# Opening and convolution of a two-layer diffusion backbone: new order of turns, two modulation chunks on VectorE, taps of two tiles in turn

## The chip, the cores and the metric

The kernel runs on one core of a Trainium2 chip. The metric is the device time of one execution in microseconds; three runs of the kernel before took 1659.43 to 1661.87 us, median 1660.55 us.

## What is computed

One sample with 512 latent tokens and 256 context tokens, D_MODEL = 1024, fp32, passes two layers. This case touches the start of layer 0: the modulation from the conditioning vector, the normalised and modulated input, the combined input projection and the depthwise convolution.

```python
silu_c = jax.nn.silu(c); silu_cc = jax.nn.silu(c_ctx)
mod = jnp.split((silu_c @ ada_w[l] + ada_b[l])[:, None, :], 6, axis=-1)      # 1024 x 6144 weights
mod_c = jnp.split(silu_cc @ ada_w[l] + ada_b[l], 6, axis=-1)
h = modulate(rms_norm(x, mix_pre_g[l]), mod[0], mod[1])                      # h * (1 + scale) + shift
hc = modulate(rms_norm(xc, mix_pre_g[l]), mod_c[0], mod_c[1])
p = h @ w_in; pc = hc @ w_in                                                 # conv | gates | q, k, v, o

def conv_module(glu_in, dw_w, ln_g, ln_b):
    a, b = jnp.split(glu_in, 2, axis=-1)
    u = a * jax.nn.sigmoid(b)
    u = dwconv(u, dw_w)                      # 31 taps, depthwise, over positions
    u = layer_norm(u, ln_g, ln_b)
    return jax.nn.silu(u)
```

The mLSTM group, the attention layer and two ConvFFNs follow; the change leaves their work as it is.

## The kernel before, in words

The program is raw: each engine (SP for the DMA queue, TensorE, ScalarE, VectorE, GpSimd) has its own list of instructions, written out by hand, and counting semaphores order them. An engine runs its list strictly in order, so an instruction that waits holds all that are behind it.

**High and low parts.** Products in fp32 are made of three matmuls: each operand is split into a high part (ScalarE, `take_high` for weights) and the rest (VectorE, `take_low`), and the matmuls are high x high, high x low, low x high. A weight granule is 128 x 4 x 256 values, 512 KB. It is loaded into one of two slots of `raw` (`load` waits until the granule two before has its low part), split into one of four slots of `w_hi` and `w_lo`, and used. `product` takes two granules (k = 0 to 3, then 4 to 7) and is one unit: two 128-column tiles over all 768 tokens. ScalarE splits granules n+4 and n+5 once the unit of granules n and n+1 is through. The semaphore `low` counts finished low parts, and `product` waits on it for each granule.

**The opening.** SP loads identity, c and c_ctx, six token tiles of x, and eight chunks `ada_0` of 1 MB each (1024 rows x 256 columns of the modulation weights) into a ring of six; ScalarE issues 19 small DMAs for vectors (`vrows`) before it does anything else. TensorE turns the vectors first (L816), then for each token tile j it turns the normalised tile (8 transposes, L816) and sums chunk j (`ada_0_sums`, L838, 16 matmuls with cond as weights), then chunks 6 and 7. Two chunks give a pair p of k-tiles with shift and scale; ScalarE copies their row (`ada_0_rows`, L1313), TensorE turns it into columns (`ada_0_cols`). ScalarE squares x and takes roots (L1178, L1181), VectorE normalises (`x_normed`, L1649, L1651) and copies the turned tokens out of PSUM (L1830). Then, pair by pair, VectorE makes the modulation vectors (L1595, L1858) and scales xT in place (L1864, four instructions a pair), ScalarE takes the high part (L1318), GpSimd the low part (L2282), and the first product waits for each k by `h0_ready`. VectorE's first `unit_low(0)` stands behind the third pair.

**The input projection.** The units are conv (4), gate (1, half width), qkov (7), two for turns, o (1). Beside the first four VectorE does `ada_sums` for two more chunks of the modulation (L1610, L1616). `gate_inputs` multiplies two tiles by the sigmoid. `conv_tile` is 31 instructions over 783 positions of one 128-channel tile (L1888, then L1890 30 times); each reads what the one before wrote and waits for it, and at given taps a `unit_low` for coming granules stands between. The rows of the mLSTM gates are scanned between tiles 1 and 2 (L1909 to L1931, ending in `rows_ready`, on which SP waits before it stores them and loads on).

## Time and profile before

| | |
|---|---|
| median of three runs | 1660.55 us |
| profiled execution | 1657.77 us, span 1656.1 us |
| TensorE matmul / weight load | 1606.8 us (97%) / 1345.1 us (81%) |
| VectorE | 1032.6 us (62%) |
| ScalarE | 552.9 us (33%) |
| GpSimd | 39.0 us (2%) |
| DMA | 169.43 MB, mean 102 GB/s |
| first matmul of the input projection | 59.44 us |

Times in the profile are microseconds from the span's start. PE is TensorE, PEld its weight load, DVE VectorE, ACT ScalarE, POOL GpSimd, SP the queue that issues DMAs. The profiled execution is one execution, 2.8 us under the median of the others; the span is the part of it that the trace covers.

### The profile page before, as it was taken

Reading aid. Unit: us, or ns where it says so; the run is one execution under the profiler, and the core shown is the slowest. Engines: PE = TensorE matmul, PEld = TensorE weight load, DVE = VectorE, ACT = ScalarE, POOL = GpSimd, SP = SyncE. Lnnn points to the kernel's source line nnn. Section 1 sums busy time; section 2 is a strip of 40 time slices with the busy share of each in tenths; the row PEclk is TensorE's granted clock in tenths of the full one; section 3 lists DMA queues with packets and bytes.
Section 4 is the critical chain, followed back from the end, with each engine's and each line's share of the span. In section 5 each row is a group of like instructions: output and inputs, shape, how many; then the busy total and the mean of one; then the engine's idle time right before and its main releaser. Section 6 shows DMA issues by size and latency. Waiting matters only on the chain.

```text
span 1656.1 us, 21947 instructions
## 1 busy us (share of the span) xinstructions
PE 1606.8 (97%) x8698; PEld 1345.1 (81%) x8698; DVE 1032.6 (62%) x1477; ACT 552.9 (33%) x883; POOL 39.0 (2%) x64
## 2 busy tenths in 40 slices
PE   5999999999999999999999999899999999999998
PEld 2688888777898887888888887788887988888886
DVE  2899996668747775566725446754885544454345
ACT  3313123665643221122311224622326432232133
POOL 0500000110000000000000000000000000000000
PEclk9999999999999999999999999999999999999999
DMA  9321212325116552456324222130002233223222
GB/s 311 129 76 53 78 51 70 115 96 127 39 51 209 179 185 87 140 166 203 117 86 140 77 77 77 55 127 26 1 11 80 89 102 115 79 88 114 88 92 85
DMA packets 134009, 169.43 MB, mean 102 GB/s; under 512 B 15970, under 2 KB 92450, under 8 KB 133930
## 3 DMA queue, kind: packets, MB, share of 16 engines
q1 hardware_dynamic: 133360, 168.11, 31.8%
q8 instruction: 55, 0.90, 0.2%
q10 hardware_dynamic: 570, 0.22, 0.1%
q14 instruction: 24, 0.20, 0.0%
HBM read 166.17 MB, written 2.15 MB: 102 GB/s over the span
## 4 chain that ended last, share of the span: by engine, by line
PE 88%; DVE 5%; ACT 3%; issue 1%; DVEq 0%; POOL 0%; ACTq 0%
PE acc L702 49%; PE acc L751 22%; PE acc L728 4%; PE acc L1135 2%; PE acc L915 2%; PE acc L1066 2%; PE acc L816 1%; PE acc L950 1%; PE acc L1081 1%; PE acc L670 1%; DVE w_lo L1595 1%; PE acc L894 1%; PE acc L742 0%; DVE h_lo L1595 0%; PE acc L1024 0%
## 5 line engine op out<-in xcount | busy, mean ns | idle before, releaser
L702 PE MATMUL acc<-h_hi,w_hi 128*128 128x512 f32 (+1 forms) x1424 | 417.3, 354 | 7.2 <-DVE w_lo L1595 4.2
L702 PE MATMUL acc<-h_lo,w_hi 128*128 128x512 f32 (+1 forms) x1424 | 413.0, 351 | 0.0
L702 PE MATMUL acc<-h_hi,w_lo 128*128 128x512 f32 (+1 forms) x1424 | 412.3, 351 | 0.0
L1595 DVE TENSOR_TENSOR w_lo<-raw,w_hi 128x1024 fp32r<-128x1024 f32 x183 | 219.7, 1230 | 147.0 <-ACT w_hi L1155 147.0
L702 PEld LDWEIGHTS acc<-h_hi,w_hi 128*128 128x128 f32 x1424 | 230.7, 189 | 45.0 <-issue 7.8
L702 PEld LDWEIGHTS acc<-h_lo,w_hi 128*128 128x128 f32 x1424 | 231.2, 189 | 38.6 <-issue 0.5
L702 PEld LDWEIGHTS acc<-h_hi,w_lo 128*128 128x128 f32 x1424 | 230.2, 189 | 38.1
L1155 ACT ACTIVATE w_hi<-raw 128x1024 fp32r<-128x1024 f32 x183 | 186.6, 1055 | 223.1 <-PE acc L751 173.9
L751 PE MATMUL acc<-w_hi,hid_hi 128*128 128x512 f32 x440 | 175.8, 400 | 0.0
L751 PE MATMUL acc<-w_lo,hid_hi 128*128 128x512 f32 x440 | 174.9, 397 | 0.0
L751 PE MATMUL acc<-w_hi,hid_lo 128*128 128x512 f32 x440 | 174.9, 397 | 0.0
L1890 DVE SCALAR_TENSOR_TENSOR conv_u<-conv_u,dw_w 128x783 f32<-128x783 f32 x120 | 124.2, 1035 | 4.0
L2118 DVE TENSOR_SCALAR hid<-gpad,ffn_cw 128x512 f32 (+1 forms) x66 | 25.2, 438 | 123.5 <-ACT gpad L1491 123.5
L751 PEld LDWEIGHTS acc<-w_hi,hid_lo 128*128 128x128 f32 x440 | 83.2, 189 | 20.4
L751 PEld LDWEIGHTS acc<-w_lo,hid_hi 128*128 128x128 f32 x440 | 83.3, 189 | 19.9
L751 PEld LDWEIGHTS acc<-w_hi,hid_hi 128*128 128x128 f32 x440 | 83.3, 189 | 19.9
L1595 DVE TENSOR_TENSOR hid<-hid,acc 128x1024 f32 (+3 forms) x22 | 32.7, 1488 | 107.1 <-ACT mods L1171 55.2
L2116 DVE SCALAR_TENSOR_TENSOR hid<-gpad,ffn_cw,hid 128x512 f32 (+3 forms) x132 | 77.6, 658 | 0.0
L1171 ACT ACTIVATE mods<-acc,vec 128x1 f32 (+2 forms) x72 | 14.4, 262 | 183.1 <-PE acc L670 183.1
L1491 ACT ACTIVATE gpad<-acc 128x1024 f32<-128x1024 f32 (+1 forms) x33 | 28.0, 887 | 118.0 <-PE acc L702 94.3
L751 PE MATMUL acc<-w_hi,h_hi 128*128 128x512 f32 x160 | 63.6, 397 | 1.0 <-DVE w_lo L1595 1.0
L751 PE MATMUL acc<-w_hi,h_lo 128*128 128x512 f32 x160 | 62.5, 390 | 0.0
(249 smaller groups left out, 2036.2 us busy)
## 6 DMA issues: line engine op xcount, KB each, us to landing
ada_w<-in_ada_w SPq DMA_DIRECT2D x88, 512.0 KB, 5.7
raw<-in_ffn_w_in SPq DMA_DIRECT2D x88, 512.0 KB, 3.7
raw<-in_ffn_w_out SPq DMA_DIRECT2D x44, 512.0 KB, 4.2
raw<-in_even_w_in SPq DMA_DIRECT2D x24, 512.0 KB, 4.5
ada<-in_ada_w SPq DMA_DIRECT2D x8, 1024.0 KB, 12.1
raw<-in_odd_w_in SPq DMA_DIRECT2D x12, 512.0 KB, 4.2
raw<-in_even_w_out SPq DMA_DIRECT2D x8, 512.0 KB, 4.7
ada_m<-in_ada_w SPq DMA_DIRECT2D x8, 512.0 KB, 4.3
```

Source lines behind the costliest of these rows:

```text
L702: last = nc.tensor.matmul(acc[:, s, m, t0:t1], w[:, slot, kk, c], x_[:, k, t0:t1], start=(k == 0 and q == 0), stop=(k == KD - 1 and q == 2))
L728: last = nc.tensor.matmul(acc[:, s, m, t0:t1], w_of(m_)[w][:, kk, c], x_[:, k, t0:t1], start=(k == 0 and q == 0), stop=(k == KD - 1 and q ...
L751: last = nc.tensor.matmul(tile_bank(name, a, j), x_[:, k, j * P:(j + 1) * P], w[:, m_ % 4, 2 * kk:2 * kk + 2, :].rearrange("p a c -> p (a ...
L915: last = nc.tensor.matmul(dst, probs[e % 4][:, t * P - t0:t * P - t0 + P], v_tok[:, ORDER[q], hd, :], start=(q, d, t) == FIRST_TOUCH[b], s ...
L1066: last = nc.tensor.matmul(acc[:, 0, n % 2, t0:t1], inb[:, 2 + hd, i * P:(i + 1) * P], kT[:, hd // 3, t0:t1], start=True, stop=True)
L1135: last = nc.tensor.matmul(acc[:, 1, 1, c:c + P], v1[:, j, (hd // 3) * HD:(hd // 3 + 1) * HD], pT[:, n % 2, j * P:(j + 1) * P], start=(j == ...
L1155: nc.scalar.activation(dst, raw[:, n % 2], ACT.Copy).then_inc(high, 1)
L1491: last = nc.scalar.activation(gpad[:, :, c:c + t1 - t0], acc[:, u % 2, :, t0:t1], ACT.Copy)
L1595: return nc.vector.tensor_tensor(out_, in0, in1, op)
L1890: ins = nc.vector.scalar_tensor_tensor(dst, src, tap, dst, ALU.mult, ALU.add)
L2116: ins = nc.vector.scalar_tensor_tensor(dst, src, c, dst, ALU.mult, ALU.add)
L2118: ins = nc.vector.tensor_scalar(dst, src, c, None, ALU.mult)
```

## The change

In the opening:
- ScalarE issues the first ten vector DMAs, SP the other nine, behind x. TensorE turns the vectors after the fourth token, into columns of the ada bank; ScalarE takes them out later (`take_vectors`).
- TensorE turns tokens 0 and 1, sums chunk 0, turns 2 and 3, sums chunk 1, turns the vectors and tokens 4 and 5, and then does chunks 4, 5, 6, 7. Chunks 2 and 3 (pair 1) are summed over k by VectorE (`ada_1_sums`, 32 instructions of 128x256 in two alternating chains) and reduced over partitions by eight one-column matmuls (`ada_1_cols`). The load order is 0, 1, 2, 4, 3, 5, 6, 7; the last comes behind the first granule of w_even. Pair 3's columns are turned inside the first product, ahead of k = 1.
- ScalarE in place of VectorE copies the turned tokens out of PSUM, one instruction a token.
- VectorE scales xT into tiles of its own (`h_32`), and ScalarE makes the high part from the unscaled xT, with shift and scale in the same instruction, two a k. VectorE in place of GpSimd makes the low part (`first_low`). `take_high` and `take_low` of the first two granules stand one by one between them.
- GpSimd clears only the pads of conv_u.

In the convolution `conv_pair` takes the taps of two tiles in turn; each instruction waits for the one before the last. The positions of the `unit_low` calls follow, with 16 now behind the row scans. One tile's result goes to a tile of its own (`conv_e`), and h_tok and sq_junk move to other addresses.

The diff, cut to its core (the helpers `take_vectors` and `turn_token` hold the moved copies and transposes; in the rest of the diff `conv_t[t]` replaces `conv_u[:, t]`):

```diff
+OPENING = (0, 1, 2, 4, 3, 5, 6, 7)
...
+        conv_e = place("conv_e", [P, U_LEN], offset=W_EDGE + 1024)
+        conv_t = [conv_u[:, 0, :], conv_e[:, :], conv_u[:, 1, :], conv_u[:, 2, :]]
+        h_tok = place("h_tok", [P, NT, P], offset=(U0 + 3 * U_LEN * 4 + 31) // 32 * 32)
...
+        def load_vectors(eng, first, end):
+            for q in range(first, end):
+                block_, src = vectors[q]
+                r = sum(v.shape[0] for b, v in vectors[:q] if b == block_)
+                eng.dma_start(vrows[r:r + src.shape[0], block_, :], src).then_inc(sem("vec_in"), 16)
...
+            load_vectors(sp, 10, N_VECTORS)
             def load_ada_0(first, end):
-                for o in range(first, end):
+                for pos in range(first, end):
+                    o = OPENING[pos]
                     c = o // 2 + 4 * (o % 2)
-                    if o >= 6:
-                        sp.wait_ge(ada0_sums, o - 5)
-                    sp.dma_start(ada_0[:, o % 6], w_ada[0][:, :, c * 256:(c + 1) * 256]).then_inc(ada0_in[o], 16)
-            load_ada_0(0, 6)
+                    if pos >= 6:
+                        sp.wait_ge(ada0_sums, pos - 5)
+                    sp.dma_start(ada_0[:, pos % 6], w_ada[0][:, :, c * 256:(c + 1) * 256]).then_inc(ada0_in[o], 16)
+            load_ada_0(0, 7)
             n = G["conv"]
...
             load(sp, n, w_even[:, 0:4, 512:768])
-            load_ada_0(6, 7)
+            load_ada_0(7, 8)
             load(sp, n + 1, w_even[:, 4:8, 512:768])
-            load_ada_0(7, 8)
...
+            def turn_vectors():
+                pe.wait_ge(sem("vec_in"), 16 * N_VECTORS)
+                for b, (n, col) in enumerate(((92, 0), (84, 92), (66, 176), (66, 242), (124, 308))):
+                    last = transpose(acc[:, v % 2, 0, 512 + col:512 + col + n], vrows[0:n, b, :], n)
+                last.then_inc(unit_done, 1)
...
+            def ada_1_cols():
+                pe.wait_ge(ada1_sums, 1)
+                psum_free(pe, v)
+                for c in range(2):
+                    for q in range(2):
+                        for x_ in range(2):
+                            at_ = 512 + 4 * c + 2 * q + x_
+                            last = nc.tensor.matmul(acc[:, v % 2, 0, at_:at_ + 1], ada_p1[:, x_, c, q * P:(q + 1) * P],
+                                                    ones[:, 0:1], start=True, stop=True)
+                last.then_inc(ada1_cols, 1)
...
+            turn_token(0)
+            turn_token(1)
+            ada_0_sums(0)
+            turn_token(2)
+            turn_token(3)
+            ada_0_sums(1)
+            turn_vectors()
+            turn_token(4)
+            turn_token(5)
+            ada_0_cols(0)
+            ada_0_sums(4)
+            ada_0_sums(5)
             ada_0_sums(6)
             ada_0_cols(2)
             ada_0_sums(7)
-            ada_0_cols(3)
+            ada_1_cols()
             h = (h_hi, h_lo)
+            def first_ready(k):
+                if k == 1:
+                    ada_0_cols(3)
+                pe.wait_ge(h0_ready, k + 1)
             for j in range(4):
-                product(pe, U["conv"] + j, G["conv"] + 2 * j, h, always if j else lambda k: pe.wait_ge(h0_ready, k + 1),
+                product(pe, U["conv"] + j, G["conv"] + 2 * j, h, always if j else first_ready,
...
+            def turned_token(j):
+                u = U["xt"]
+                if j < NT - 1:
+                    act.wait_ge(xt_full, j + 1)
+                else:
+                    psum_full(act, u)
+                nc.scalar.activation(xT[:, :, j * P:(j + 1) * P], acc[:, u % 2, j % 2, :].rearrange("p (k t) -> p k t", k=KD),
+                                     ACT.Copy).then_inc(xt_taken if j < NT - 1 else set_free[u % 2], 1)
...
+            def ada_0_rows(p):
+                act.wait_ge(ada0_sums, (2, 0, 4, 6)[p])
+                if p:
+                    act.wait_ge(ada0_cols, p - 1)
+                c = 512 * (p % 2)
+                nc.scalar.activation(ada_r[0:2, :], acc[0:2, U["ada"] % 2, p // 2, c:c + 512], ACT.Copy).then_inc(ada0_rows, 1)
+            def first_high(p):
+                act.wait_ge(mods0, p + 1)
+                for k in (2 * p, 2 * p + 1):
+                    for s_, (t0, t1) in enumerate(SEGS[T]):
+                        last = nc.scalar.activation(h_hi[:, k, t0:t1], xT[:, k, t0:t1], ACT.Identity,
+                                                    bias=mods[:, 0, 0, k, s_:s_ + 1], scale=mods[:, 0, 1, k, s_:s_ + 1])
+                    last.then_inc(t_high, 1)
...
+                if j >= 2:
+                    turned_token(j - 2)
             ada_0_rows(0)
-            ada_0_rows(1)
+            take_vectors()
+            turned_token(NT - 2)
+            turned_token(NT - 1)
+            psum_read(act, U["xt"])
             first_high(0)
             ada_0_rows(2)
+            take_high(0)
+            ada_0_rows(3)
+            take_high(1)
             first_high(1)
-            unit_high(0)
-            ada_0_rows(3)
             first_high(2)
             first_high(3)
             unit_high(2)
...
+            def ada_1_sums(e):
+                o = 2 + e
+                dve.wait_ge(ada0_in[o], 16)
+                for k in range(KD):
+                    for x_ in range(2):
+                        w, scale, of = ada_0[:, OPENING.index(o) % 6, k, :], cond[:, k, x_:x_ + 1], ada_p1[:, x_, e, :]
+                        if not k:
+                            ins = nc.vector.tensor_scalar(of, w, scale, None, ALU.mult)
+                        else:
+                            sd.wait(sd.value() - 1)
+                            ins = nc.vector.scalar_tensor_tensor(of, w, scale, of, ALU.mult, ALU.add)
+                        if e and k == KD - 1 and x_:
+                            ins.then_inc(ada1_sums, 1)
+                        else:
+                            sd.done(ins)
...
+            def first_mods(p):
+                u = U["ada"]
+                k = slice(2 * p, 2 * p + 2)
+                if p == 3:
+                    psum_full(dve, u)
+                elif p == 1:
+                    dve.wait_ge(ada1_cols, 1)
...
-                        last = nc.vector.tensor_scalar(xT[:, kk, t0:t1], xT[:, kk, t0:t1], mods[:, 0, 1, kk, s:s + 1],
+                        last = nc.vector.tensor_scalar(h_32[kk][:, t0:t1], xT[:, kk, t0:t1], mods[:, 0, 1, kk, s:s + 1],
                                                        mods[:, 0, 0, kk, s:s + 1], ALU.mult, ALU.add)
                     last.then_inc(t_ready, 1)
-                if p == 2:
-                    unit_low(0)
+            def first_low(p):
+                for k in (2 * p, 2 * p + 1):
+                    dve.wait_ge(t_ready, k + 1)
+                    dve.wait_ge(t_high, k + 1)
+                    vt(h_lo[:, k, :], h_32[k][:, :], h_hi[:, k, :].bitcast(F32), ALU.subtract).then_inc(h0_ready, 1)
+            for j in range(NT):
+                if j >= 2:
+                    dve.wait_ge(xt_full, j - 1)
+                x_normed(j, j)
+            psum_read(dve, U["cond"])
+            ada_1_sums(0)
+            psum_read(dve, U["vec"])
+            psum_read(dve, U["xt"])
+            first_mods(0)
+            ada_1_sums(1)
+            first_low(0)
+            take_low(0)
+            first_mods(1)
+            first_low(1)
+            first_mods(2)
+            first_low(2)
+            take_low(1)
+            first_mods(3)
+            first_low(3)
             unit_low(2)
...
-            def conv_tile(t, lows):
+            def conv_pair(t, lows):
                 dve.wait_ge(sem("sig_used"), t // 2 + 1)
-                dst = conv_u[:, t, HALF:HALF + taps_len]
+                sd.wait()
                 for w in range(TAPS):
-                    src = conv_u[:, t + 1, w:w + taps_len]
-                    sd.wait()
-                    tap = dw_w[:, w, t:t + 1]
-                    if w == 0:
-                        ins = nc.vector.tensor_scalar(dst, src, tap, None, ALU.mult)
-                    else:
-                        ins = nc.vector.scalar_tensor_tensor(dst, src, tap, dst, ALU.mult, ALU.add)
-                    sd.done(ins)
                     if w in lows:
                         unit_low(lows[w])
+                    for t_ in (t, t + 1):
+                        src, dst = conv_u[:, t_ + 1, w:w + taps_len], conv_t[t_][:, HALF:HALF + taps_len]
+                        tap = dw_w[:, w, t_:t_ + 1]
+                        if w == 0:
+                            sd.done(nc.vector.tensor_scalar(dst, src, tap, None, ALU.mult))
+                        else:
+                            sd.wait(sd.value() - 1)
+                            sd.done(nc.vector.scalar_tensor_tensor(dst, src, tap, dst, ALU.mult, ALU.add))
                 sd.wait()
             ada_sums(EVEN[0], sums_even[0])
             ada_sums(EVEN[1], sums_even[1])
             psum_read(dve, U["conv"] + 1)
             gate_inputs(0)
-            conv_tile(0, {2: 6, 13: 8, 30: 10})
+            conv_pair(0, {0: 6, 9: 8, 15: 10, 21: 12, 28: 14})
             psum_read(dve, U["conv"] + 3)
             gate_inputs(2)
-            conv_tile(1, {8: 12, 20: 14, 30: 16})
...
-            unit_low(18)
-            conv_tile(2, {13: 20, 29: 22})
-            conv_tile(3, {13: 24, 29: 26})
+            unit_low(16)
+            conv_pair(2, {4: 18, 13: 20, 21: 22, 29: 24})
             nc.vector.tensor_copy(mark[:, 2:3], ident[:, 0:1]).then_inc(sem("conv_done"), 1)
+            unit_low(26)
...
-                pool.wait_ge(t_high, k + 1)
-                nc.gpsimd.tensor_tensor(h_lo[:, k, :], xT[:, k, :], h_hi[:, k, :].bitcast(F32), ALU.subtract).then_inc(h0_ready, 1)
             pool.wait_ge(h0_ready, KD)
-            nc.gpsimd.memset(conv_u[:, :, :], 0.0).then_inc(sem("conv_zero"), 1)
+            for first, end in ((0, U_LAT), (U_LAT + LAT, U_CTX), (U_CTX + CTX, U_LEN)):
+                ins = nc.gpsimd.memset(conv_u[:, :, first:end], 0.0)
+            ins.then_inc(sem("conv_zero"), 1)
```

## Rows read from the trace of the kernel before

**Rows 1.** The page, totals and the chain that ended last.
```profile
PE 1606.8 (97%) x8698; PEld 1345.1 (81%) x8698; DVE 1032.6 (62%) x1477; ACT 552.9 (33%) x883; POOL 39.0 (2%) x64
...
PE 88%; DVE 5%; ACT 3%; issue 1%; DVEq 0%; POOL 0%; ACTq 0%
```

**Rows 2.** Table by stage: each engine's busy time, granted clock, DMA.
```profile
core 0: us, PE busy (x) PEld busy (x) DVE busy (x) ACT busy (x) POOL busy (x), PEclk, DMA share, GB/s
17.89:59.44 41.55, 38.37 (x193) 17.75 (x193) 24.65 (x42) 15.47 (x27) 8.57 (x5) 1.00 0.57 183
59.44:78.20 18.76, 18.76 (x97) 16.21 (x98) 16.73 (x17) 3.52 (x4) 12.65 (x5) 0.91 0.75 242
78.20:259.50 181.30, 181.30 (x1041) 157.56 (x1040) 174.20 (x183) 46.22 (x51) 0.00 (x0) 1.00 0.23 69
62.00:63.00 1.00, 1.00 (x4) 0.81 (x4) 0.96 (x2) 0.00 (x0) 1.00 (x2) 0.50 1.00 338
```

**Rows 3.** Timeline of TensorE: start, length, instruction, count, idle before and releaser.
```profile
16.02 0.98 PE L816 MATMUL acc<-ident,vrows 92*128 92x92 f32 x5 [12.26 <-DMA vrows<-in_conv_dw_w]
...
19.79 5.24 PE L838 MATMUL acc<-ada,cond 128*2 128x256 f32 x16
24.96 1.09 PE L816 MATMUL acc<-ident,xn 128*128 128x128 f32 x8
25.99 3.61 PE L838 MATMUL acc<-ada,cond 128*2 128x256 f32 x16
...
44.93 7.07 PE L838 MATMUL acc<-ada,cond 128*2 128x256 f32 x32
```

**Rows 4.** The chain in order of time: start, length, engine and line.
```profile
57.04 2.40 issue
59.44 35.69 PE acc L702 x192
95.12 1.68 PE acc L670 x16
```

**Rows 5.** Timeline of VectorE, 46 to 60 us.
```profile
46.83 1.65 DVE L1864 TENSOR_SCALAR xT<-xT,mods 128x512 f32<-128x512 f32 x4
...
48.78 4.55 DVE L1864 TENSOR_SCALAR xT<-xT,mods 128x512 f32<-128x512 f32 x4
...
58.12 2.35 DVE L1595 TENSOR_TENSOR w_lo<-raw,w_hi 128x1024 fp32r<-128x1024 f32 x2
```

**Rows 6.** DMA from 0 to 75 us in 40 slices, and x's loads.
```profile
GB/s 2 109 349 363 407 409 345 325 333 348 348 347 348 349 348 348 348 348 348 351 321 81 0 0 0 0 4 0 0 4 0 0 175 347 357 399 366 227 145 225
...
L480 SPq DMA_DIRECT2D x<-in_ctx x2: 504/514/524, 3.8 to 4.4; - x2
...
DMA to landing us min/median/max: 4.3/6.7/9.2
```

**Rows 7.** ScalarE: a copy out of PSUM, grouped, and squares from the timeline.
```profile
L1345 ACT ACTIVATE conv_u<-acc 128x1024 f32<-128x1024 f32 x2 | 2.1, 1038 | 13.1 <-PE acc L702 13.1
...
19.08 1.04 ACT L1178 ACTIVATE junk<-x 128x1024 f32<-128x1024 f32 x1
...
20.45 1.04 ACT L1178 ACTIVATE junk<-x 128x1024 f32<-128x1024 f32 x1
```

**Rows 8.** VectorE: groups (count, busy us, mean ns) and timeline of ada chains and taps.
```profile
L1890 DVE SCALAR_TENSOR_TENSOR conv_u<-conv_u,dw_w 128x783 f32<-128x783 f32 x120 | 124.2, 1035 | 4.0
...
L1616 DVE SCALAR_TENSOR_TENSOR ada_c<-ada_w,cond,ada_c 128x512 f32<-128x512 f32 x28 | 19.3, 747 | 0.6
...
87.23 9.94 DVE L1616 SCALAR_TENSOR_TENSOR ada_c<-ada_w,cond,ada_c 128x512 f32<-128x512 f32 x14
...
105.95 11.75 DVE L1890 SCALAR_TENSOR_TENSOR conv_u<-conv_u,dw_w 128x783 f32<-128x783 f32 x11
```

**Rows 9.** Timelines of VectorE and ScalarE around the convolution.
```profile
99.00 1.97 DVE L1595 TENSOR_TENSOR conv_u<-conv_u,sig_b 128x512 f32<-128x512 f32 x4 [1.83 <-ACT conv_u L1345]
...
182.04 0.94 DVE L1909 SCALAR_TENSOR_TENSOR rows<-rows 8x768 f32<-8x768 f32 x1
...
195.12 2.34 DVE L1595 TENSOR_TENSOR w_lo<-raw,w_hi 128x1024 fp32r<-128x1024 f32 x2
...
191.69 1.46 ACT L1369 ACTIVATE qkov<-acc 128x1536 f32<-128x1536 f32 x1 [13.61 <-PE acc L702]
```

137 lines of the change are left out of this document (41 added, 96 removed).

## Prediction

> **What bounds the kernel now.** The page's totals come first [rows 1]: the reader is to see TensorE busy for 97% of the span and the chain that ended last lying on it for 88%. Work taken from another engine counts only where TensorE stands and waits for it. The table by stage says where that is [rows 2]: from 17.89 to 59.44 us TensorE is nearly full (38.37 of 41.55), but with preparation; from 59.44 us on, in the first input product, and from 78.20 to 259.50 us it has no idle time at all. So what happens before the first product moves the end one for one, unless later work comes too late for TensorE.
>
> The timeline of TensorE [rows 3] shows the preparation: vector turns at 16.02 us after 12.26 us of waiting for the last vector's DMA, token turns of 1.03 us (24.96 to 25.99), and eight modulation chunks of 3.54 us each (two in 7.07). The chain [rows 4] has 2.40 us put down to issue just ahead of the first product. VectorE's first w_lo ends them (58.12 [rows 5] plus one of two at 1.18 us gives 59.3), so the last step is not TensorE's. VectorE's own rows [rows 5] say why it is late: four scalings take 1.65 us at 46.83 and 4.55 us at 48.78, when GpSimd works on h_lo.
>
> **The opening, step by step, in the order of the new program.**
> ScalarE issues 10 vector DMAs in place of 19, so it starts some 3 us earlier; SP issues the other nine behind x, while x is still arriving. Tokens 0 and 1 are turned at about 10 to 14 us. Then TensorE waits for the first ada chunk. The DMA rate is flat at 348 GB/s [rows 6]; x, identity and vectors are 3.44 MB, so the first chunk's bytes are through at 15.5 us, and x itself landed some 1.4 us behind its bytes (the last at most 9.2 us after an issue at 4.4): I take 17.
>
> From there TensorE's list, with the prices of rows 3: first chunk 5.2 (as slow as now), two turns 2.1, second chunk 3.55, vectors 1.0, two turns 2.1, four row transposes 0.35, chunks o = 4, 5, 6 10.65, transposes 0.35, chunk 7 3.55, and eight column matmuls for the pair computed on VectorE, 0.85 (16 take 1.68 [rows 4]). Sum 29.7, hence 46.7 us. Two chunks (7.1 us) are gone, the waits at both ends besides. The last chunk's bytes are through at 38.2 us by the same rate, with w's first granule in front: not limiting by 4 us or more, and the two ring waits on SP are met at 22 and 28 us while DMA still has over 3 us queued.
>
> Do the others keep up? ScalarE now copies the turned tokens: 128x1024 out of PSUM is 1.04 us, squares with root 1.37 us per token (19.08 to 20.45) [rows 7]. Its copy of token 2 ends at 24.5, squares of token 5 at 26, token 5's xn at 27.1, before TensorE wants it at 30. VectorE loses its copies out of PSUM and gets 32 partial-sum steps on 128x256. No row has this shape. The same operation on 128x512 in two alternating chains takes 0.71 us start to start (14 in 9.94) [rows 8]; 271 more elements cost 0.288 us (1035 against 747 ns), so 256 fewer make 0.44; the first step of each chain is a tensor_scalar, 0.31 as an estimate under the 0.41 that one of 384 columns takes on average at 46.83 [rows 5]. A chunk is 14 x 0.44 + 2 x 0.31 = 6.8 us; the bounds are 5 us (at 0.3 a step) and 11.4 us (at the 512 price). VectorE: first chunk 27.2 to 34.0, modulation and four scalings to 36.0 (1.65 us, since GpSimd now has no h_lo), second chunk to 42.8, first_low(0) two at 0.9 to 44.7, first take_low to 45.9. That is 0.8 us before TensorE's 46.7, the tightest meeting of the opening. ScalarE's take_high(0) follows the rows at 38.4 and ends at 40.
>
> Then products: k = 0 to 48.8, the last row transposes (0.35), k = 1 to 51.3. Meanwhile VectorE gets the pair's columns at 46.7 and has k = 2's low part at 49.7, 3's at 50.6, 4's at 53.4, 5's at 54.4, and take_low(1) at 55.6, which the second half of the product wants at 55.5: 0.1 us. Parts 6 and 7 come at 58.5 and 59.4, wanted at 59.8 and later. ScalarE's affine high parts run beside VectorE's scalings instead of behind them; 512 and 256 columns at some 0.95 us a k (three quarters of the 1.04, and a second start) stay ahead of first_low. Without a stall this product takes 17.0 us plus 0.4; now it takes 18.76, of which the surplus is a stretch at the lower clock: the granted clock was 0.50 (1.2 GHz) at 62 us [rows 2], behind 2.40 us in which TensorE stood. The new order leaves no such stand. So product 0 ends at 64.1 instead of 78.20: **14.1 us gained**. GpSimd's memset of the pads alone, after 59.4, is hidden: ScalarE asks for it at 64.
>
> **The convolution.** It is all on VectorE, off the path; what counts is when each w_lo between the taps is ready. Per tap now: 11 in 11.75, 1.068 us start to start, with each waiting for the one before. The alternating ada chains start 0.037 us ahead of the previous duration's end (0.71 against 747 ns) where the serial taps start 0.033 behind (1.068 against 1035 ns) [rows 8]. I take 1.00 for a tap in turn; bounds 0.95 and 1.07. 124 taps give back 8 us of VectorE, which buys nothing by itself.
>
> The Trainium skill ("VectorE: DVE Perf Modes", section "The DRAIN you can't avoid") says the flush behind each operation can't be skipped by dropping semaphores, which would make a tap in turn cost what a serial one does. Rows 8 already show two prices for the two ways of waiting, and the sum goes by them. By the page the conv term would be that of the first rival below.
>
> Now count from the end of the second product (now 96.8, then 82.7). VectorE leaves the opening at 62.3 (w_hi 3 waits for its load), does two ada_sums at 10.8 and a pair of w_lo at 2.35, and begins gate_inputs at +3.5, where it now begins at +2.2 (99.00) [rows 9]. Then gate_inputs 1.97, w_lo 6 and 7 2.35, 18 steps, w_lo 8, 12 steps, w_lo 10, 12 steps, w_lo 12, 14 steps, w_lo 14, 6 steps: +78.4. Each of these comes 1 us or more ahead of its product. Then gate_inputs 1.97 and the row scans 13.1 (182.04 to 195.12) [rows 9], and only now unit_low(16), which stood ahead of the scans until now: granule 16 is ready at +94.6, and its product starts at +94.9 (191.69 less 96.8). Margin 0.3 us, with the sum above uncertain by two; I count 0.3 us of stall. Later ones (18 at +102, 20 at +123, 22 at +142) meet 111.9, 128.9 and 145.8; the last, 26, waits for ScalarE as it does now. The loads behind them follow each w_lo by less than 9.2 us, the slowest landing of the 512 KB transfers in rows 6, and rows_ready, on which SP stands, comes 5 us earlier against the products (+93 for +98). From 260 us on nothing changes but places of tiles.
>
> **Sum.** 14.1 - 0.3 = 13.8 us. The profiled execution took 1657.77 us with a span of 1656.1; it becomes 1644.0. It lies 2.8 us below the median of the runs, so for the median: 1660.55 - 13.8 = **1646.8 us**.
>
> **Rivals.**
> *Taps gain nothing* (13%). Then granule 16 is late by 60 x 0.07 - 0.3 = 3.9 us, once, before the fourth qkov product; 14.1 - 3.9 = 10.2, hence 1650.4. For it: no row has taps in turn with these tiles. Against: rows 8.
> *VectorE bounds the opening* (9%). If a 128x256 step costs what a 128x512 one does, both chunks take 22.8 for 13.6 us, the first w_lo comes at 55.1, and 8.4 us of the gain are gone: 5.4 left, 1655.2. For it: no row has the shape. Against: 271 elements more cost 288 ns [rows 8].
> *TensorE stays at its lower clock* (6%), the case that ends slower. The first chunk takes 5.24 us where later ones take 3.61 [rows 3]; and in product 0 the granted clock fell to 0.50 behind a stand [rows 2]. The new order interrupts TensorE before the first chunk and puts short transposes between. A chunk at half the clock costs 3.5 us more; four of them use up the 14 us, and from there the kernel is slower: five chunks make 17.5, and with a third of product 0 (17 us more if all of it is at half the clock) 23, hence some 1670; 1665 in the middle of the case. Against: from 24.4 on there is no gap longer than those of now, where chunks took 3.54.
> *The gain is given back at a later wait* (3%), no change: nothing between 78 and 260 us shows a wait that doesn't move along.
>
> **How the numbers follow.** The forecast has 69%, with 1644 to 1649 as its own range: 1.6 us for the first chunk all at the slow pace, 2 for take_low's meetings and arrival of ada, 1.4 for the taps' margin, 1 for the median. The range goes to 1642.5 below (no stall, 1 us from earlier ada, scatter of runs of 1.2) and to 1653.5 above, which takes in the taps' case and part of the second. A measurement of this kernel can tell 0.2%, 3.3 us, from no change. Faster by more: forecast, taps, and nearly all of the second rival, 0.90; the same 0.04; slower 0.06.
>
> **What would show it.** In the new profile: the first L702 matmul at 46 to 48 us; six chunks with 3.5 us each behind the first; a granted clock of 1.00 through the first product, which lasts 17.4 us; 32 steps on VectorE at 0.44; taps at 1.00 start to start; a TensorE wait for w_lo of 0 to 1 us before the fourth qkov product; all that follows as long as before. I am wrong if that wait is 4 us, if the first product stands at k = 2 or 4, or starts after 50 us.

## The result, and the profile after

Kernels run together on one chip gave 1648.64 us (median of four runs, 1647.59 to 1650.08) for the changed kernel and 1660.41 us (1659.43 to 1661.87) for the one before: a ratio of 0.9935, 95% interval 0.9922 to 0.9948, or 11.8 us less. The forecast was 13.8 us less.

The page of the changed kernel, totals and the chain that ended last:
```profile
PE 1605.0 (97%) x8678; PEld 1349.0 (82%) x8678; DVE 1022.0 (62%) x1505; ACT 561.6 (34%) x896; POOL 18.0 (1%) x58
...
PE 91%; DVE 5%; ACT 2%; issue 1%; DMA 1%; SPq 0%; DVEq 0%; POOL 0%; ACTq 0%
```
Against [rows 1] TensorE's busy time is nearly the same; its share of the chain rose from 88 to 91%. VectorE is 10.6 us less busy and GpSimd 21 us less, and neither number says anything of the gain.

The table by stage, with the borders moved to where the same work stands now:
```profile
core 0: us, PE busy (x) PEld busy (x) DVE busy (x) ACT busy (x) POOL busy (x), PEclk, DMA share, GB/s
17.22:46.66 29.44, 29.44 (x158) 14.48 (x158) 18.73 (x45) 12.09 (x21) 0.00 (x0) 0.94 0.88 279
46.66:64.69 18.03, 18.03 (x104) 15.27 (x104) 17.26 (x32) 9.54 (x14) 0.36 (x3) 1.00 0.46 162
64.69:245.98 181.29, 181.29 (x1042) 157.66 (x1040) 175.65 (x196) 46.02 (x51) 0.00 (x0) 1.00 0.26 76
```
The third row is the comparison to begin with: 181.29 us here, 181.30 us for the same stretch in [rows 2], at 1.00. From the first product's end to the last qkov copy nothing was gained or lost. The gain lies ahead of it: the preparation takes 29.44 us and starts at 17.22, and TensorE has no idle time in it; the first product takes 18.03 where it took 18.76, at a granted clock of 1.00 for 0.91.

TensorE's timeline from the first token turns to the first product:
```profile
10.48 3.65 PE L843 MATMUL acc<-ident,xn 128*128 128x128 f32 x16 [6.65 <-DVE xn L1704]
17.22 5.30 PE L874 MATMUL acc<-ada,cond 128*2 128x256 f32 x16 [3.09 <-DMA ada<-in_ada_w]
22.45 1.97 PE L843 MATMUL acc<-ident,xn 128*128 128x128 f32 x16
24.35 3.61 PE L874 MATMUL acc<-ada,cond 128*2 128x256 f32 x16
27.90 0.60 PE L843 MATMUL acc<-ident,vrows 92*128 92x92 f32 x5
28.34 1.91 PE L843 MATMUL acc<-ident,xn 128*128 128x128 f32 x16
...
30.52 10.52 PE L874 MATMUL acc<-ada,cond 128*2 128x256 f32 x48
...
41.30 3.62 PE L874 MATMUL acc<-ada,cond 128*2 128x256 f32 x16
44.85 1.95 PE L894 MATMUL acc<-ones,ada_p 128*128 128x1 f32 x16
46.66 0.59 PE L729 MATMUL acc<-h_hi,w_hi 128*128 128x512 f32 x2
```
Read it by the starts; lengths overlap a little. There are six chunks of the modulation (16 + 16 + 48 + 16 matmuls) where [rows 3] had eight, and the only two waits stand ahead of 17.22. The first product, which stood at 59.44 [rows 4], starts at 46.66.

VectorE in the same time, with its two chunks:
```profile
26.94 0.61 DVE L1882 TENSOR_SCALAR ada_p<-ada,cond 128x256 f32<-128x256 f32 x2
27.46 5.63 DVE L1885 SCALAR_TENSOR_TENSOR ada_p<-ada,cond,ada_p 128x256 f32<-128x256 f32 x14
...
35.49 5.62 DVE L1885 SCALAR_TENSOR_TENSOR ada_p<-ada,cond,ada_p 128x256 f32<-128x256 f32 x14
...
42.77 1.22 DVE L1648 TENSOR_TENSOR w_lo<-raw,w_hi 128x1024 fp32r<-128x1024 f32 x1
46.83 0.17 DVE L1648 TENSOR_TENSOR mods<-acc,vec 128x8 f32<-128x8 f32 x1 [2.85 <-PE acc L894]
```
A step costs 0.40 us (5.63 / 14), and the first w_lo ends at 44.0, 2.7 us before TensorE asks. The [2.85 <-PE] in the last row says who leads: VectorE waits for TensorE's columns, not the other way.

The convolution's taps, and the pair of w_lo behind the row scans:
```profile
90.80 1.03 DVE L1969 SCALAR_TENSOR_TENSOR conv_u<-conv_u,dw_w 128x783 f32<-128x783 f32 x1
91.74 1.03 DVE L1969 SCALAR_TENSOR_TENSOR conv_e<-conv_u,dw_w,conv_e 128x783 f32<-128x783 f32 x1
92.69 1.03 DVE L1969 SCALAR_TENSOR_TENSOR conv_u<-conv_u,dw_w 128x783 f32<-128x783 f32 x1
...
173.44 2.34 DVE L1648 TENSOR_TENSOR w_lo<-raw,w_hi 128x1024 fp32r<-128x1024 f32 x2
```
A tap starts every 0.946 us (90.80 to 92.69 is two), against 1.068 in [rows 8], though one instruction is still recorded as 1.03 us. Granule 16 is ready at 174.65, one of the two in the last row.

ScalarE's copies of the qkov products show TensorE's pace, and when that granule is wanted:
```profile
178.14 1.46 ACT L1422 ACTIVATE qkov<-acc 128x1536 f32<-128x1536 f32 x1 [13.62 <-PE acc L729]
195.10 1.46 ACT L1422 ACTIVATE qkov<-acc 128x1536 f32<-128x1536 f32 x1 [13.54 <-PE acc L729]
```
The product with granule 16 begins where a copy begins, at 178.1: a margin of 3.5 us, and no wait for w_lo.

**Where the difference sits.** The same instruction on both traces, changed less before: first product's start -12.8 us, its end -13.5, every qkov copy from 144 to 246 us -13.6, the last copy of the stage (o, at 273.19) -13.7, then -12.0 at the first FFN's entry, -8.9 in layer 1 and to the end (the span -8.6). (The mark called o is ScalarE's copy of the last product of the stage.) The opening's gain reached 273 us whole, and 5 us of it seemed to be lost in two stages in which the change moves only the places of some tiles. That needed the first two runs.

### The profile page after: what moved, and what is told of

Same layout as the page of the kernel before. It is cut to its first block, busy times and chain, and to the rows that moved or that the text cites. A ratio compares the mean times of both kernels' runs of the same rounds, so it can differ in the third digit from the quotient of the medians.

```text
span 1647.5 us, 21953 instructions
## 1 busy us (share of the span) xinstructions
PE 1605.0 (97%) x8678; PEld 1349.0 (82%) x8678; DVE 1022.0 (62%) x1505; ACT 561.6 (34%) x896; POOL 18.0 (1%) x58
## 4 chain that ended last, share of the span: by engine, by line
PE 91%; DVE 5%; ACT 2%; issue 1%; DMA 1%; SPq 0%; DVEq 0%; POOL 0%; ACTq 0%
PE acc L729 49%; PE acc L778 22%; PE acc L755 4%; PE acc L970 2%; PE acc L1190 2%; PE acc L1121 2%; PE acc L843 2%; PE acc L874 1%; PE acc L1136 1%; PE acc L1005 1%; PE acc L697 1%; PE acc L983 1%; DVE w_lo L1648 1%; PE acc L949 1%; DMA ada<-in_ada_w 1%
## 5 line engine op out<-in xcount | busy, mean ns | idle before, releaser
L1969 DVE SCALAR_TENSOR_TENSOR conv_u<-conv_u,dw_w 128x783 f32<-128x783 f32 x90 | 87.8, 1020 | 0.0
## 6 DMA issues: line engine op xcount, KB each, us to landing
ada<-in_ada_w SPq DMA_DIRECT2D x8, 1024.0 KB, 11.8
```

Source lines behind the costliest of these rows:

```text
L1969: sd.done(nc.vector.scalar_tensor_tensor(dst, src, tap, dst, ALU.mult, ALU.add))
```

## The experiments

Twelve runs. `before_again` and `after_again` are the two kernels unchanged; the others are the changed kernel with the edit shown.

**1. Are the two late stages a loss?** (`before_again`)

> The kernel before, unchanged, profiled a second time. Theory 1 (the stretches at the lower TensorE clock fall and last differently in each execution): ratio 1.000 within 0.1%; the trace shows the same instructions at the same distances, but the summed time at a granted clock of 0.5, 28.6 us in the first trace, differs by 5 us or more, and the span follows it by half. Theory 2 (each kernel has its own stretches): the same stretches at the same places to 1 us, 28.6 us in sum.

Measured: 1660.76 us (ten runs), ratio 0.9998 [0.9988, 1.0007] to its own comparison runs; this trace has a span of 1660.6 us. The attention stage of layer 1 in three traces, the first kernel twice and then the changed one:
```profile
1071.50:1302.47 230.97, 222.97 (x1338) 186.55 (x1337) 153.01 (x247) 88.48 (x156) 0.00 (x0) 0.99 0.17 53
```
```profile
1072.55:1306.99 234.44, 226.45 (x1338) 189.30 (x1337) 153.03 (x247) 88.42 (x155) 0.00 (x0) 0.97 0.17 52
```
```profile
1059.54:1293.56 234.02, 226.02 (x1338) 189.23 (x1337) 153.08 (x247) 88.44 (x155) 0.00 (x0) 0.97 0.17 52
```
The counts are the same and the busy times of VectorE and ScalarE too; TensorE is 3.5 us longer busy in the second trace of the *unchanged* kernel, at 0.97 for 0.99. So the 3.0 us that the change seemed to cost there belong to the first trace of before, which was 2.6 us under the median of its runs. The time at the lower level of the clock (granted 0.50, 1.2 GHz) can be added up from the granted clock of windows of 2 us over the whole span: 28.7 us in that trace, 47.7 in this one, 45.8 in the changed kernel's (the next expectation has 47.9 for it). So the sum differed by 19 us between two executions of one kernel, well over the least 5 that was expected, but the span grew by 4.5 us, a quarter of that and not half.

**2. The changed kernel once more** (`after_again`)

> The changed kernel, unchanged, profiled a second time and timed in five rounds. Theory 1: ratio 0.9925 to 0.9935 (11 to 12.5 us), the sum at the lower clock, 47.9 us in the first trace, comes out nearer 35, and the span falls by half the difference; the first 277 us gain 13.6 as in the first trace. Theory 2 (the new kernel has more stretches of its own and gives 2 to 5 us back by them): 47.9 us again, at the same places.

Measured: 1649.62 us, 0.9934 [0.9921, 0.9948]; first product at 46.63, its end at 64.67, o at 273.33: the opening repeats within 0.2 us. The time at the lower clock, added up in the same way, was 48.1 us, not the smaller sum expected: that part missed.

**3. The opening alone** (`opening_only`): the taps one tile at a time, as before.
```diff
-            def conv_pair(t, lows):
+            def conv_tile(t, lows):
...
-            conv_pair(0, {0: 6, 9: 8, 15: 10, 21: 12, 28: 14})
+            conv_tile(0, {2: 6, 13: 8, 30: 10})
```

> The new opening with the old convolution: one tile after the other, each tap waiting for the last, the low parts at their old places. My theory: the opening carries the whole gain, the first product starts at 46.6 us, the end of the third qkov product is 13.6 us earlier than before; ratio within 0.05% of the changed kernel's. Granules 16 and 17 are then split ahead of the row scans: no wait of TensorE. Rival (the faster taps carry part, since VectorE comes later to the convolution): a wait of TensorE for w_lo of 1 to 4 us between 120 and 250 us, ratio 0.1 to 0.25% above the changed kernel's.

Measured: 1649.65 us, 0.9934 [0.9921, 0.9948], the whole change's ratio to the last digit. TensorE meets the end of the convolution late, though:
```profile
259.47 1.53 PE L949 MATMUL acc<-conv_u,ones 128*128 128x512 f32 x4 [1.40 <-DVE small L2011]
```
No wait was expected here, so that part missed, and it is tempting to call these 1.4 us what the faster taps buy. But this trace had TensorE at a faster pace (see the last section): its last qkov copy stands at 244.38 us, against 245.98 in the changed kernel, where the same matmul starts at 259.35 without a wait. VectorE let it go here at 259.47. At the changed kernel's pace some 0.1 us of the wait would be left, so that the taps buy next to nothing there, and o stands at 273.24 and 273.19 in the two traces.

**4. The convolution alone** (`conv_only`): the opening as before.
```diff
-            load_vectors(sp, 10, N_VECTORS)
...
-                for pos in range(first, end):
-                    o = OPENING[pos]
+                for o in range(first, end):
```

> The old opening with the new convolution: taps of two tiles in turn. My theory: taps start every 0.946 us instead of 1.068, VectorE has 15 us more, and the time stays as before: ratio 1.000 within 0.1%, since no low part was waited for before. Rival (VectorE's freed time or the moved low parts reach the path): a ratio below 0.999, or above 1.001 if granule 16, now behind the row scans, comes late for its product at 191.7 us.

Measured: 1661.31 us (eleven runs), 1.0002 [0.9993, 1.0011], and no TensorE wait at all from 60 to 259 us. A tap starts every 0.946 us here too, so 120 of them take some 15 us less of VectorE's time than at 1.068, in a stretch where TensorE never waited for it: nothing. Runs 3 and 4 together put the whole gain in the opening.

**5. All eight chunks on TensorE** (`chunks_on_pe`): the pair computed on VectorE goes back.
```diff
-OPENING = (0, 1, 2, 4, 3, 5, 6, 7)
+OPENING = (0, 1, 2, 3, 4, 5, 6, 7)
...
+            ada_0_sums(2)
+            ada_0_sums(3)
...
-                ada_1_cols()
```

> The changed kernel with all eight modulation chunks summed by TensorE, as before: chunks 2 and 3 and their columns stand behind the vector turns, the load order is 0 to 7. My theory (the opening is TensorE's list, and the pair on VectorE takes 7.1 us of it and gives 1.95 back by its columns): the first product starts 5.0 to 5.8 us later, at 51.7 to 52.5 us, and all later marks with it. Rival (VectorE's and ScalarE's chain sets the start, so that the pair on VectorE bought nothing): start at 46 to 48 us.

Measured: 1652.85 us (ten runs), 0.9955 [0.9942, 0.9969].
```profile
17.53 6.24 PE L874 MATMUL acc<-ada,cond 128*2 128x256 f32 x16 [3.32 <-DMA ada<-in_ada_w]
...
25.60 3.62 PE L874 MATMUL acc<-ada,cond 128*2 128x256 f32 x16
...
53.43 0.62 PE L729 MATMUL acc<-h_hi,w_hi 128*128 128x512 f32 x2
```
From the second chunk's start to the first product it is 27.83 us here and 22.31 (24.35 to 46.66) in the changed kernel: 5.52 us. That is two chunks at 3.55 and a set of row transposes at 0.33, less 1.81 for the eight column matmuls: 5.6. The rest of the later start, 1.25 us, is the first chunk, which came 0.3 us later and ran 0.9 us longer. In all the product starts 6.8 us later, where 5.0 to 5.8 were expected. Of the 12.8 us by which the first product starts earlier, 5.5 are the pair's; the other 7.3 belong to the rest of the new opening: no 12-us wait with a late preparation behind it, and no 2.40 us ahead of the product. No run takes those edits apart. In the medians the pair is worth 3.2 us (1652.85 and 1649.62), and at o 3.7: this trace ran its later products at 16.64 us each and not 16.96, which gave part of the late start back.

**6. Each tap waits for the last one again** (`pair_waits_last`), in the new order and with the new places.
```diff
-                            sd.wait(sd.value() - 1)
+                            sd.wait()
```

> The changed kernel; each tap of a pair waits for the instruction just before it instead of the one before the last. My theory (what a tap in turn saves is the wait for its forerunner's end): taps start every 1.068 us again instead of 0.946; the low part of granule 16 then comes 5.7 us later (7.3 less the 1.65 us that VectorE now waits for w_hi at 119.6) and TensorE waits some 2.3 us for it before the fourth qkov product at 178.1 us. Rival (the flush behind each VectorE instruction is paid either way, and the gain per tap came from the other tile's addresses): taps stay at 0.946 and no wait appears.

Measured: 1652.31 us in one run. VectorE, then TensorE at granule 16:
```profile
91.31 1.04 DVE L1969 SCALAR_TENSOR_TENSOR conv_u<-conv_u,dw_w 128x783 f32<-128x783 f32 x1
92.38 1.03 DVE L1969 SCALAR_TENSOR_TENSOR conv_e<-conv_u,dw_w,conv_e 128x783 f32<-128x783 f32 x1
```
```profile
180.46 0.60 PE L729 MATMUL acc<-h_hi,w_hi 128*128 128x512 f32 x2 [3.69 <-DVE w_lo L1648]
...
182.46 0.84 PE L729 MATMUL acc<-h_lo,w_hi 128*128 128x512 f32 x2
183.10 0.84 PE L729 MATMUL acc<-h_hi,w_lo 128*128 128x512 f32 x2
```
The step went from 0.946 to 1.070 us with nothing changed but which predecessor is waited for: 0.124 us a tap. And the first rival's mechanism exists: granule 16 is 3.69 us late, and behind the wait pairs of matmuls start 0.64 us apart for some 3 us, where they start 0.35 apart otherwise. The wait was expected shorter (2.3): TensorE came 1.3 us earlier, since it ran at the faster pace up to there (the copy before stands at 176.81, not 178.14); at the changed kernel's pace the wait would be some 2.4. The time of the one run can't show a loss of this size.

**7. GpSimd takes the opening's low parts again** (`low_on_gpsimd`).
```diff
-            first_low(0)
...
+            for k in range(KD):
+                pool.wait_ge(t_ready, k + 1)
+                pool.wait_ge(t_high, k + 1)
+                nc.gpsimd.tensor_tensor(h_lo[:, k, :], h_32[k][:, :], h_hi[:, k, :].bitcast(F32), ALU.subtract).then_inc(h0_ready, 1)
```

> The changed kernel with the first low parts on GpSimd, from the same scaled tiles. My theory (GpSimd beside VectorE slows both): VectorE's partial sums of the second chunk, 0.40 us a step, go to 0.6 or more while GpSimd works, and GpSimd's 1.9 us a k becomes 2.3 to 2.8 beside VectorE; the first product starts 0 to 2 us later and ends 1 to 4 us later. Rival (the move to VectorE bought nothing): both marks within 0.3 us of the changed kernel's 46.65 and 64.2 us.

Measured: 1649.4 us in one run; first product at 46.94, and it takes 19.44 us (18.03 in the changed kernel), with two waits in it, 0.7 for w_lo and 0.6 for h_lo. VectorE, then GpSimd:
```profile
35.25 3.73 DVE L1882 TENSOR_SCALAR ada_p<-ada,cond 128x256 f32<-128x256 f32 x2
38.90 5.62 DVE L1885 SCALAR_TENSOR_TENSOR ada_p<-ada,cond,ada_p 128x256 f32<-128x256 f32 x14
...
50.92 4.67 DVE L1916 TENSOR_SCALAR h<-xT,mods 128x512 f32<-128x512 f32 x4
```
```profile
35.20 3.63 POOL L2348 TENSOR_TENSOR h_lo<-h,h_hi 128x768 fp32r<-128x768 f32 x2 [34.26 <-ACT h_hi L1360]
```
Two tensor_scalars that take 0.61 us alone take 3.73 beside GpSimd's pair, which runs from 35.20 to 38.83: they end as it ends. The four scalings go from 1.65 to 4.67, as in [rows 5]. The long chain behind them keeps its 0.40 a step, so the slower steps that were expected there missed. Taking GpSimd out of the opening is worth 1.4 us in the first product by this trace; in the time of one run it doesn't show.

**8. The high parts from the scaled tiles** (`high_from_scaled`): ScalarE copies h_32 when VectorE has scaled it.
```diff
-                    for s_, (t0, t1) in enumerate(SEGS[T]):
-                        last = nc.scalar.activation(h_hi[:, k, t0:t1], xT[:, k, t0:t1], ACT.Identity,
...
+                    act.wait_ge(t_ready, k + 1)
+                    nc.scalar.activation(h_hi[:, k, :], h_32[k][:, :], ACT.Copy).then_inc(t_high, 1)
```

> The changed kernel; ScalarE takes the high part as a copy of the scaled tile, one instruction a k behind VectorE's scaling, instead of two with shift and scale from the unscaled tile. My theory (0.81 us a copy keeps pace with 0.82 us of scaling a k; the low part comes when it did): start and end of the first product within 0.3 us of the changed kernel's. Rival (the edit shortens the chain to h_lo by a scaling): the first product waits at k = 2 for 0.5 to 1 us and ends as much later.

Measured: 1652.38 us in one run. The first product takes 18.25 us, 0.2 more, with the same 0.3 us of wait for w_lo; it starts 0.6 us later, for a first chunk that took 6.14 us. The edit is worth between 0 and 0.2 us.

**9. Spare work ahead of the first chunk** (`warm`): 30 and 28 transposes of the identity into a bank nobody reads, ahead of token 0's turns and behind token 1's.
```diff
+            def warm(n):
+
+                for q in range(n):
+                    transpose(acc[:, v % 2, 1, 512:640], ident[:, :])
+
+            warm(30)
...
+            warm(28)
```

> The changed kernel with 30 spare 128x128 transposes of the identity on TensorE ahead of token 0 and 28 between token 1 and the first chunk, where it stands idle for 6.6 and 3.1 us. My theory (the first chunk takes 5.3 us in place of 3.6 because TensorE comes to it at its lower clock): turns of 1.03 us and a first chunk of 3.6 us, and the first product starts 1.4 to 1.7 us earlier than at 46.65. Rival (the first chunk is slow for its data still arriving, or TensorE's start is bounded elsewhere): 5.3 us again, or a start within 0.3 us.

Measured: 1645.96 us in one run; the first and the last chunk, and the product:
```profile
17.38 3.62 PE L874 MATMUL acc<-ada,cond 128*2 128x256 f32 x16 [0.51 <-DMA ada<-in_ada_w]
...
40.58 3.61 PE L874 MATMUL acc<-ada,cond 128*2 128x256 f32 x16 [0.73 <-DMA ada<-in_ada_w]
...
45.93 0.59 PE L729 MATMUL acc<-h_hi,w_hi 128*128 128x512 f32 x2
```
A TensorE that turned spare tiles up to 0.51 us before the first chunk, instead of standing for 3.09, runs it in 3.62 us instead of 5.30: what TensorE did before sets the price. In the changed kernel the granted clock agrees, 0.67 over the chunk (here 1.00), but not in every trace. The first chunk in the changed kernel and in `opening_only`:
```profile
17.22:22.45 5.23, 5.23 (x16) 1.63 (x16) 0.00 (x0) 0.00 (x0) 0.00 (x0) 0.67 1.09 348
```
```profile
17.59:23.70 6.11, 6.11 (x16) 1.79 (x16) 0.00 (x0) 0.00 (x0) 0.00 (x0) 1.00 1.09 348
```
The second is slower still, at a recorded 1.00, as are `chunks_on_pe` (6.17) and `high_from_scaled` (6.07), and the kernel before took 5.17 us at 1.00. So the run shows that the slow chunk comes from the stand; that the lower clock is all of it is not shown. Less came through (0.7 us): the last chunk's load, ordered behind w's first granule and a ring wait, is now what TensorE waits for.

**10. The first chunk ahead of x's last tokens** (`ada_early`).
```diff
+                if j == 2:
+                    load_ada_0(0, 1)
```

> The changed kernel with the first ada chunk loaded ahead of x's third tile instead of behind all of x and the vectors. My theory (the opening is TensorE's list from the first chunk's landing on): the first chunk starts at 14 us in place of 17.2, and what follows moves up by 3 us until the last chunk's landing (39.6 us) stops it: its sum starts at about 39.7 in place of 41.3, the first product at 45.1, 1.5 us earlier. Rival (another chain bounds the start): within 0.3 us of 46.65.

Measured: 1647.73 us in one run.
```profile
13.42 3.62 PE L874 MATMUL acc<-ada,cond 128*2 128x256 f32 x16
...
20.53 3.61 PE L874 MATMUL acc<-ada,cond 128*2 128x256 f32 x16 [1.60 <-DMA ada<-in_ada_w]
...
32.53 8.76 PE L874 MATMUL acc<-ada,cond 128*2 128x256 f32 x32 [2.22 <-DMA ada<-in_ada_w]
```
Starting 3.8 us earlier gained nothing: TensorE outruns the loads, waits 1.60 and 2.22 us, and behind the second the clock falls again (0.80 over the two chunks, which take 8.76 us for 7.07). The product starts at 46.91: the expected 45.1 was missed by 1.8.

**11 and 12. Both, and spare work with the last chunk's load first.** `early_order_warm` joins 9 and 10 and takes VectorE's chunk 3 after 5; `warm_last_first` is run 9 with
```diff
-            load_ada_0(0, 7)
+            load_ada_0(0, 8)
...
-            load_ada_0(7, 8)
```

> The changed kernel with three edits: the first ada chunk ahead of x's third tile, load order 0, 1, 2, 4, 5, 3, 6, 7 with both granules of w behind the last chunk, and 30 spare transposes ahead of token 0. My theory (landing times and TensorE's list share the bound): chunk 6 is summed from 35 us, chunk 7 to 42.3, the first product starts at 44.1 us, 2.5 us earlier than in the changed kernel, ratio 0.991 to 0.993. Rival (short waits for chunks 1 and 5 bring the lower clock back): chunks of 5 us or more behind these waits and a start after 46 us.

> The changed kernel with the 58 spare transposes of the previous run and with the last ada chunk loaded ahead of both granules of w instead of between them. My theory (the 0.73 us for which TensorE waited for the last chunk at 39.8 us goes, nothing else is late): chunk 7 starts behind its forerunners without a wait, the first product at 45.2 us, 1.4 us earlier than in the changed kernel; in time that is too little to show beside executions that differ by 2 us either way: ratio 0.991 to 0.994. Rival (the first granule of w, now later, holds the first product): a wait for w_lo and a start at 46 us or later.

Measured: `early_order_warm` 1650.01 us (six runs, 1646.94 to 1654.42), 0.9933 [0.992, 0.9947], first product at 45.34 (44.1 expected) with waits of 1.44 and 2.29 us for DMA on the way. The rival, chunks of 5 us behind these waits, didn't come:
```profile
36.11 3.62 PE L873 MATMUL acc<-ada,cond 128*2 128x256 f32 x16 [2.29 <-DMA ada<-in_ada_w]
```
So a stand of 2.29 us cost nothing here, where 2.22 us in `ada_early` cost 1.7; what makes the difference isn't shown. `warm_last_first` gave 1649.32 (1646.77 to 1650.83), 0.9926 [0.9913, 0.994]:
```profile
39.85 3.62 PE L873 MATMUL acc<-ada,cond 128*2 128x256 f32 x16
...
45.20 0.59 PE L728 MATMUL acc<-h_hi,w_hi 128*128 128x512 f32 x2
```
The last chunk doesn't wait, and the product starts at 45.20, as the sum had it: 1.4 us earlier than in the changed kernel, the earliest of all. In the time it can't be told from it (0.9926 and 0.9934, intervals overlapping). Its own trace shows a reason, behind o, at a load that the changed kernel's TensorE meets without waiting:
```profile
292.93 1.35 PE L989 MATMUL acc<-cond,ada_m 128*128 128x2 f32 x8 [1.31 <-DMA ada_m<-in_ada_w]
```
It came to o 1.29 us ahead of the changed kernel (271.90 and 273.19) and waits 1.31 us here; at the first FFN's entry nothing is left (487.18 and 487.13). In `early_order_warm` this wait is 0.28 us. That trace, the slowest of its six executions, has something larger in the same stage:
```profile
292.00:304.00 12.00, 11.98 (x50) 10.29 (x51) 3.82 (x6) 1.23 (x2) 0.37 (x2) 0.58 0.39 124
```
TensorE full for 12 us, with 50 matmuls at a granted clock of 0.58. The stage took 218.22 us in place of 213.94: such a stretch costs more than the opening had left to give.

Marks of the traces, in us (pace: from one qkov copy to the next; the last three are lengths from o on: to the first FFN, the two FFN stages with what is between, the attention stage):
```
kernel             product 0 starts  ends    pace    o        lengths
before                  59.44        78.24   16.96   286.90   212.20 572.40 230.97
before_again            58.97        77.50   16.96   285.69   212.92 573.94 234.44
conv_only               58.20        76.73   16.64   282.68   211.78 574.00 233.85
chunks_on_pe            53.43        70.99   16.64   276.93   212.04 573.97 234.45
opening_only            47.91        65.80   16.64   273.24   212.01 572.39 233.99
after                   46.66        64.69   16.96   273.19   213.94 572.41 234.02
after_again             46.63        64.67   16.96   273.33   213.73 574.75 234.00
warm                    45.93        63.97   16.96   272.62   214.30 572.40 230.93
early_order_warm        45.34        63.37   16.96   272.02   218.22 573.96 234.51
warm_last_first         45.20        63.24   16.96   271.90   215.28 573.99 233.95
```

## Why the prediction was right, step by step

**What bounds.** Right. What ended before the first product moved everything behind it up to o; the 181.29 us after it stayed to the hundredth. Runs 3 and 4 show the same from outside: opening alone 0.9934, convolution alone 1.0002.

**The first product's start: 46.7 expected, 46.66 measured.** The terms didn't all hold; their errors cancel, so that the match to 0.04 us is luck. From start to start: wait for the first chunk to 17.22 (17); first chunk 5.23 (5.2); two turns 1.90 (2.1); second chunk 3.55 (3.55); vectors 0.44 (1.0); two turns 1.84 (2.1); row transposes 0.34 and 0.33 (0.35); three chunks 10.45 (10.65); the last 3.55 (3.55); columns 1.81 (0.85). The mis-sized term is the last. Eight fp32 matmuls against a column of ones are 16 instructions in the trace, and they take 1.81 us, near the 1.68 that [rows 4] gave for 16: the row was there, but the count was taken from the source. The vectors' 1.0 came from a record's length (0.98), when what counts is the distance to the next start.

**VectorE: step 0.40, not 0.44**; a chunk 6.1 us, not 6.8; first take_low at 44.0, not 45.9. The second rival (9%), that VectorE bounds the opening, is out: it waits 2.85 us for TensorE. The loads were no limit in the change itself, but closer to one than counted: in run 9 the last chunk's data let TensorE go at 40.58, 0.7 us ahead of that chunk's start in the changed kernel (41.30), where the forecast had over 4 us (38.2 by bytes).

**Product 0: 17.4 expected, 18.03 measured.** 16.96 is the product, 0.33 the row transposes, 0.30 a wait for take_low(1) at 55.87 (0.1 was expected at 55.5), and 0.44 remains: some 0.3 for three restarts (after the columns, the row transposes and the wait), whose first pair of matmuls takes about 0.1 longer each (0.59 to 0.62, not 0.51), and 0.15 that no row explains. The granted clock was 1.00 as forecast: without the 2.40-us stand, no fall at 62 us. The third rival (6%) didn't come: chunks behind the first took 3.5. Its mechanism is real nevertheless: runs 6, 9 and 10 show 1.5 to 1.7 us behind a stand of 2 to 4 us. It isn't a fixed price, since in `early_order_warm` a stand of 2.29 us cost nothing.

So the term was 14.1 and came out at 13.5: the product's extra 0.6.

**The convolution: 0.3 us of stall expected, none measured.** The tap was taken at 1.00, between 0.95 and 1.07, and is 0.946. Sixty steps by 0.054 make the 3.2 us by which granule 16 beat the forecast (ready 91.4 us behind the second product's end, not 94.6). Whoever adds up the 62 steps of the forecast at 1.00 gets 79.2 and not its 78.4; it comes out with the two first steps, tensor_scalars, at some 0.6, which the forecast doesn't say. The first rival (13%) is settled by run 6, which is that rival built: a tap of 1.070 and a late granule, 3.69 us against the 3.9 in its sum. That the two are so near is luck again, since the pace of that trace made the wait 1.3 us longer. The rule of the Trainium skill that was weighed there ("VectorE: DVE Perf Modes", section "The DRAIN you can't avoid") would have priced both ways of waiting alike; here 0.946 and 1.070 us stand for the same 128x783 operation, so for taps the measurement decides against reading the rule that way. That section of the Trainium skill says besides that a next operation that isn't held starts earlier, which leaves room for what was measured. What part of the 0.124 us is the drain and what the semaphore's way isn't shown.

**All that follows as long as before: right up to o, and behind it only within a scatter that was underrated.** Of the 13.6 us, 11.8 are in the medians. In the two later stages of the table what varies, varies in the unchanged kernel too (572.40 and 573.94, 230.97 and 234.44), with the same counts and the same busy times of the other engines, and the lengths go with stretches at the lower clock, of which a trace has 28.7 to 55.0 us. What decides where they fall stays open.

The stage right behind o is another matter, and there the fourth rival (3%), that the gain is given back later, isn't out. It took 212.20 and 212.92 us in the two traces of the kernel before, and 213.94 and 213.73 in the two of the changed kernel, at a granted clock of 0.95 for 0.97 and 0.96. The other places of h_tok and sq_junk aren't the reason, since `conv_only` has them and took 211.78. The remaining variants lie between 212.0 and 218.2. So 1 to 2 us may be given back there; with two traces of each kernel it stays open. For openings that are earlier still a later wait is shown: the one of 1.31 us for ada_m in `warm_last_first`.

Against `before_again` the opening's start gained 12.3 us and o 12.5, which is nearer to the medians. The remaining difference is inside the interval (0.9922 to 0.9948 is 8.6 to 13.0 us).

## What to carry to other kernels

Count what stands between two starts on the bounding engine, and count instructions as the trace counts them. Work on another engine is worth something only where the bounding engine waits for it: the taps' edit gave back some 15 us of VectorE and no measurable time. An earlier start is worth its whole length only up to the next load or result that comes when it did before, as ada_m behind o. Before a late difference is explained, profile the kernel *before* once more: two traces of it differ here by 4.5 us in span, a third of the gain looked for.

## What the runs showed of the hardware

**Two paces at full clock.** At a granted clock of 1.00, with no wait between, the same products take 16.96 us each in some traces and 16.64 in others. ScalarE's copies of `opening_only`, to be read against those of the changed kernel above:
```profile
177.82 1.46 ACT L1422 ACTIVATE qkov<-acc 128x1536 f32<-128x1536 f32 x1 [13.29 <-PE acc L729]
194.46 1.46 ACT L1422 ACTIVATE qkov<-acc 128x1536 f32<-128x1536 f32 x1 [13.30 <-PE acc L729]
```
A pair of matmuls starts every 0.353 us at the one pace and every 0.347 at the other. A trace isn't bound to one of them, and TensorE needn't stand for a change. In `before_again` the third product runs at 0.3465 a pair (46 pairs from 96.04 to 111.98 us) and the fourth, behind 16 short matmuls, at 0.3534 (44 pairs from 115.18 to 130.73), with TensorE busy throughout:
```profile
112.33 1.84 PE L670 MATMUL acc<-ones,ada_c 128*128 128x1 f32 x16
114.04 0.61 PE L702 MATMUL acc<-h_hi,w_hi 128*128 128x512 f32 x2
```
`conv_only` has both paces among its first products too. Through the seven qkov products, which have nothing between them, each trace kept one pace, but for `pair_waits_last`: 16.64 up to the 3.69-us wait and 16.90 to 17.02 behind it. Eight products at 0.32 us are 2.6 us of scatter that no edit made, and that is what `opening_only` made up: it started 1.25 us later than the changed kernel, waited 1.40 us, and had reached it at o. What sets the pace wasn't found.

**VectorE beside GpSimd, by kind of instruction.** Two tensor_scalars went from 0.61 to 3.73 us beside GpSimd's tensor_tensor pair, and ended 0.15 us behind it; the chain of scalar_tensor_tensors directly behind it kept 0.40 a step. Whether such a chain would stretch under GpSimd isn't shown, since the pair had ended.

**The price of waiting for the last result** on VectorE: 1.070 us start to start for a 128x783 scalar_tensor_tensor that waits for its predecessor, 0.946 for one that waits for the one before it, with 1.03 recorded as the length of either.
